# Gate products of an xLSTM step with high and low weights in one stationary array, and the first two query evacuations ahead of the gate rows

## The chip, the core and the metric

The kernel is one program on one core of a Trainium2 chip. The metric is the device time of one execution in microseconds (us). TensorE (PE in the profile, with its weight loads as PEld) multiplies, VectorE (DVE) and ScalarE (ACT) do elementwise work, GpSimd (POOL) does some of it and issues a few transfers, and SyncE (SP) issues most transfers.

## The reference

A decoder step of two layers over 512 prompt tokens and 32 sample tokens (8 sequences of 4), width 1024, all in float32. Layer 0 mixes tokens with an mLSTM (8 heads), layer 1 with a short gated convolution, and each is followed by a squared-ReLU MLP. Every sub-layer has an RMS norm with shift, scale and gate from a conditioning vector (`ada_w`). What the change touches is the gate part of the mLSTM projection: 16 of the columns of `mlstm_w_in`.

```python
def mlstm_mixer(h, C0, n0, m0, w_in, b_gates, g_head, w_out):
    p = (h @ w_in).astype(jnp.float32)
    q = p[..., :hk]
    k = p[..., hk:2 * hk] * (DK_A ** -0.5)
    ...
    gates = p[..., 2 * hk + 2 * D_MODEL:] + b_gates.astype(jnp.float32)
    ig = gates[..., :H_A]
    lf = jax.nn.log_sigmoid(gates[..., H_A:])
    ...
```

The input gates `ig` and the log forget gates `lf` then go through running sums and running maxima over the tokens, which give the decay rows of every head.

## The kernel before

**Tiles.** Activations lie transposed: 8 channel blocks of 128 partitions, each with 544 columns (two halves of 272, which are 256 prompt tokens and 16 sample tokens). A product in full precision is made of three products of rounded parts. The high part of a weight tile is `wh`, the low part `wl = raw - wh`; those of the activations are `Xh` and `Xl`. A weight tile of 128 output channels is 8 channel blocks times (wh·Xh, wh·Xl, wl·Xh) times two halves, which makes 48 matmuls into one of two slots of the accumulator tensor `G`.

**Supply.** SP fetches a raw tile (512 KB) into one of two buffers, ACT rounds it (`hi`, L596) into one of four slots, and POOL subtracts (`lo`, L1102), after which the raw buffer is free for the tile two further on. The tiles of the first stage are the queries and keys, numbers 0 to 7 (T_QK); values (8 to 15), output gates (16 to 23) and so on follow.

**The head of the program.** TensorE turns the input, then makes the first products of `ada_w` (`ada_pair`, 32 small matmuls each, L2153), which give shift and scale of the first norm. DVE and ACT write `Xh` and `Xl` in two groups of four blocks. `gates(k)` (L2240) multiplies block k by the gate weights `gh` (high) and `gl` (low), each 40 columns wide with the input gates at columns 0 to 7 and the forget gates at 32 to 39; three products times two halves, into banks `B5` and `B7`. TensorE does `gates(0)` to `gates(3)`, two ada pairs, and then tiles 0 and 1 together (`head_pair`, matmuls of L1994): blocks 0 to 3 of tile 0, two ada pairs, blocks 0 to 3 of tile 1, and from block 4 on block k of both with `gates(k)` behind it. After that come one ada pair on two tiles of `aring`, tiles 2 and 3 (matmuls of L1968), one ada pair, tiles 4 and 5, and so on. The data of each of these ada pairs are refilled by ACT, which issues the transfers (L471).

**Behind the gates.** DVE adds the bias (L1606, L1607) and makes the absolute value (L1609, semaphore `s_rv`), ACT takes exponential and logarithm (L909, L910), and DVE makes the sums and maxima (L1612 to L1630, second count of `s_rv`).

**What sets the order around the change.** Each engine does its instructions in the order written. In ACT's program, behind the first norm: `hi(2)`, `hi(3)`, then the wait for `s_rv`, L909 and L910, `hi(4)`, the evacuation of tile 0 (`to_qk`, L713 and L714, which empties the slot of `G`), that of tile 1, a refill of two ada tiles, `hi(5)`. Tile 2 uses the slot of tile 0, so TensorE waits for tile 0's evacuation before it. Four tiles later `rows_prompt` waits on ACT for the second count of `s_rv`, behind the evacuation of tile 4.

Of the kernel before, what the change touches and what calls it, by code (L numbers as in the profile page):

```python
# [13 lines left out]
F32 = mybir.dt.float32  # L14
F32R = mybir.dt.float32r
ALU = mybir.AluOpType
ACT = mybir.ActivationFunctionType
AX = mybir.AxisListType

P = 128  # L20
D = 1024
KT = D // P
SEQ, SB, ST = 512, 8, 4
PH, SH = SEQ // 2, SB * ST // 2
HALF = PH + SH
# [3 lines left out]
H, DK, DV = 8, 64, 128  # L29
# [8 lines left out]
SLOTS, RAWS, ADAS, LEAD = 4, 2, 2, 3  # L38
# [12 lines left out]
T_QK, T_V, T_O, T_WOUT, T_MLP0, T_MLP0L, T_MLP0_LAST = 0, 8, 16, 24, 32, 48, 80  # L51
T_CG, T_XT, T_BG, T_COUT, T_MLP1, T_MLP1_LAST, T_END = 96, 104, 112, 120, 128, 176, 192
G_QK, G_V, G_O, G_WOUT, G_MLP0, G_MLP0L, G_MLP0_LAST = 0, 8, 16, 24, 32, 48, 80
# [87 lines left out]
def build_program(nc, ins, outs):  # L141
    ctx = ExitStack()
    with ctx:
# [3 lines left out]
        def sb(name, shape, dt=F32, at=None):  # L147
            n = 4
            for s in shape[1:]:
                n *= s  # L150
            n = (n + 31) // 32 * 32
            if at is None:
                at = mark["at"]
                mark["at"] += n
            return nc.alloc_sbuf_tensor_at(name, shape, dt, offset=at)

        def region(nbytes):
            at = mark["at"]
            mark["at"] += (nbytes + 31) // 32 * 32
            return at  # L160

        def sem(name):
            return ctx.enter_context(nc.semaphore(name))

        ROW = TOK * 4
# [16 lines left out]
        Xh = sb("Xh", [P, KT, TOK], F32R)  # L182
        Xl = sb("Xl", [P, KT, TOK], F32R)
# [38 lines left out]
        at_sq = region(6 * ROW)  # L222
# [13 lines left out]
        bgate = sb("bgate", [P, 1])  # L236
# [4 lines left out]
        xr = sb("xr", [P, TOK], at=at_n + 2 * ROW)  # L241
# [14 lines left out]
        at_f = region(2 * 4 * ROW + KT * ROW + NJ * H * DK * 4)  # L256
# [9 lines left out]
        rows_all = sb("rows_all", [H, 6, TOK], at=at_f + 8 * ROW)  # L266
        rows = [rows_all[:, i, :] for i in range(6)]
        erow = sb("erow", [H, SEQ - P], at=at_f + 14 * ROW)
        gw = 8 * 40 * 4
        graw = sb("graw", [P, KT, 40], at=at_f + 14 * ROW)  # L270
        gh = sb("gh", [P, KT, 40], F32R, at=at_f + 14 * ROW + gw)
        gl = sb("gl", [P, KT, 40], F32R, at=at_f + 14 * ROW + 2 * gw)
        crow = sb("crow", [NSEQ, D], at=at_f)
        parrow0 = sb("parrow0", [P, P], at=at_f + 12288)
        parrow1 = sb("parrow1", [40, P], at=at_f + 12288 + 512)
# [94 lines left out]
        s_gs = sem("gates_split")  # L370
# [207 lines left out]
        def _(act):  # L578
            chain = Count(act, s_a)

            def hi(t, j=None, per=0):

                if t >= T_END:
                    return
                if fast_of(t) is not None:
                    hi_group(fast_of(t)[1], 0, t - fast_of(t)[1])
                    return
                raw_wait(act, t)
                if t >= SLOTS and fast_of(t - SLOTS) is not None:
                    v, u = fast_of(t - SLOTS)  # L590
                    act.wait_ge(s_pu, NP * (PAIRS * v + 3) + min(2 * (t - u - KT) + 2, NP))
                elif t >= SLOTS:
                    act.wait_ge(s_used, at(t - SLOTS + 1, j, per))
                else:
                    act.wait_ge(s_au, 8)
                nc.scalar.activation(wh[:, t % SLOTS], raw_of(t), ACT.Copy).then_inc(s_hi, 1)  # L596
# [129 lines left out]
            def ada_next(k):  # L726

                act.wait_ge(s_au, 2 * (k + 1))
                for a in range(2 * (k + 1), min(2 * (k + 2), BATCH * KT)):
                    ada_fetch(nc.scalar, a)  # L730
# [21 lines left out]
            def raw_hi(n, k):  # L752

                act.wait_ge(s_gn, n)
                act.wait_ge(s_dr, done((0, G_WOUT, G_MLP0_LAST + 8, G_COUT)[n] + k + 1))
                nc.scalar.activation(prompt(XP[n][0][:, k, :]), prompt(xT[:, k, :]), ACT.Identity, scale=gain[:, k, 0:1])\
                    .then_inc(s_xph, 1)
# [67 lines left out]
            def mixed(t0, g0, n, evac, j=None, per_t=0, per_g=0, per_n=0, after={}, ada_after=ADA_AFTER, raws=None):  # L825

                for m in range(KT):
                    t = t0 + m
                    if t != T_QK and m != 1:
                        hi(t + LEAD, j, per_t)  # L830
                    if m == 0:
                        hi(t + 1 + LEAD, j, per_t)
                    if evac is not None:
                        evac(t, g0 + m, j, per_t, per_g)
                    if m in after:
                        after[m]()
                    if raws is not None and m:
                        raw_hi(raws, m - 1)
                    if m in ada_after:
                        ada_next(4 * n + ada_after[m])  # L840
# [47 lines left out]
            for j in range(NJ + 1):  # L888
# [4 lines left out]
                last = nc.scalar.activation(xsq[j % 2][0:n, :], xin[0:n, j, :], ACT.Square, accum_out=rms[0:n, 1, j:j + 1])  # L893
# [3 lines left out]
                nc.scalar.activation(prompt(xT[:, k, :]), G[:, k % 4, :].rearrange("p (h c) -> p h c", h=2),  # L897
                                     ACT.Copy).then_inc(s_xe, 1)
            act.wait_ge(s_gin, 80)
            nc.scalar.activation(gh[:, :, :], graw[:, :, :], ACT.Copy).then_inc(s_gs, 1)  # L900
            first_norm_hi(0)
            first_norm_hi(1)
            hi(2)
# [1 line left out]

            nc.scalar.dma_start(xspill, xT[:, :, :].rearrange("p k c -> p (k c)")).then_inc(s_spill, 16)

            act.wait_ge(s_rv, 1)
            chain.link(nc.scalar.activation(rows[1][:, :], rows[0][:, :], ACT.Exp, scale=-1.0))  # L909
            nc.scalar.activation(rows[2][:, :], rows[1][:, :], ACT.Ln, bias=1.0).then_inc(s_ra, 1)  # L910
# [152 lines left out]
            for i, bank in enumerate((B4, B6)):  # L1063
                last = nc.scalar.activation(urows[:, i * 512:(i + 1) * 512], bank[0:2 * NSEQ, :], ACT.Copy)
# [15 lines left out]
            for j, bank in enumerate((B4, B5, B6, B7)):  # L1080
                last = nc.scalar.activation(yrow[:, j, 0:HALF_D], bank, ACT.Copy)
# [140 lines left out]
        def _(dve):  # L1222
            chain = Count(dve, s_v)
            V = nc.vector
# [365 lines left out]
                                       sample(xr[:, :]).unsqueeze(1).broadcast_to((P, KT, 2, SH)), ALU.mult))  # L1590
            scaled_x(range(4))
            dve.wait_ge(s_gs, 1)
            V.tensor_tensor(gl[:, :, :], graw[:, :, :], gh[:, :, :].bitcast(F32), ALU.subtract).then_inc(s_gs, 1)
            first_norm(0)
            first_norm_low(0)
            scaled_x(range(4, KT))
# [5 lines left out]
            R = [r[:, :] for r in rows]  # L1602
            lf = sqb[0:H, :]
            for hf, bank in enumerate((B5, B7)):
                cols = slice(hf * HALF, (hf + 1) * HALF)
                V.tensor_scalar(R[3][:, cols], bank[0:H, 0:HALF], bgate[0:H, :], None, ALU.add)  # L1606
                V.tensor_scalar(R[4][:, cols], bank[32:32 + H, 0:HALF], bgate[32:32 + H, :], None, ALU.add)  # L1607
            chain.link(V.memset(xr[0:H, :], 1.0))
            V.scalar_tensor_tensor(R[0], R[4], -1.0, R[4], ALU.mult, ALU.max).then_inc(s_rv, 1)  # L1609
            dve.wait_ge(s_ra, 1)  # L1610
# [160 lines left out]
            for h2 in range(2):  # L1771
                pr = slice(DK * h2, DK * (h2 + 1))
                for b in range(SB):
                    last = V.tensor_copy(qbd[pr, :, b, NS * h2 + ST * b:NS * h2 + ST * (b + 1)], qe[pr, :, ST * b:ST * (b + 1)])
# [3 lines left out]
            for h2 in range(2):  # L1778
                pick = lambda ap: ap.rearrange("p (a h) t -> p a h t", h=2)[:, :, h2, :]
                last = V.scalar_tensor_tensor(  # L1780
                    pick(probs_s[:, :, :])[:, :, NS * h2:NS * (h2 + 1)],
                    (B7, B6)[h2][0:NS, 0:H // 2 * NS].rearrange("p (a t) -> p a t", t=NS), KS,
                    pick(dec_s[:, :, :]), ALU.mult, ALU.mult)
# [160 lines left out]
            for half, bank in enumerate((B7, B6)):  # L1944
                last = V.tensor_scalar(yrow_s[:, half * HALF_D:(half + 1) * HALF_D], bank[0:NS, :], rms[0:NS, 1, NJ:NJ + 1], None, ALU.mult)
# [4 lines left out]
        def _(pe):  # L1950
            mm = nc.tensor.matmul

            def turn(out, in_, n):
                return nc.tensor.transpose(out, in_, ident[0:n, 0:n])  # L1954
# [250 lines left out]
            for k in range(KT):  # L2205
                last = turn(B5[:, k * NSEQ:(k + 1) * NSEQ], crow[:, k * P:(k + 1) * P], NSEQ)
# [7 lines left out]
            for k in range(KT):  # L2214
                last = turn(B6[:, k * NS:(k + 1) * NS], xin[0:NS, NJ, k * P:(k + 1) * P], NS)
            last.then_inc(s_xst, 1)
            for k in range(KT):
                if k >= 4:
                    pe.wait_ge(s_xe, k - 3)
                if k == 5:  # L2220
# [4 lines left out]
                    for hf, bank in enumerate((B5, B7)):  # L2225
                        last = mm(bank[:, PH:HALF], ones[:, :], diag[:, NJ, hf * SH:(hf + 1) * SH], start=True, stop=True)
                    last.then_inc(s_root, 1)
                for jt in range(NJ):
                    last = turn(G[:, k % 4, jt * P:(jt + 1) * P], xin[:, jt, k * P:(k + 1) * P], P)
# [9 lines left out]

            def gates(k):  # L2240
                pe.wait_ge(s_kx, X_NORM0 + k + 1)
                for w, x, st, en in ((gh, Xh, k == 0, False), (gh, Xl, False, False), (gl, Xh, False, k == KT - 1)):
                    for hf, bank in enumerate((B5, B7)):
                        last = mm(bank[0:40, 0:HALF], w[:, k, :], x[:, k, hf * HALF:(hf + 1) * HALF], start=st, stop=en)
                if k == KT - 1:
                    last.then_inc(s_gp, 1)

# [219 lines left out]
            for q in range(QUARTERS - 1):  # L2467
                t, g = T_MLP0L + 16 * q, G_MLP0L + 16 * q
# [17 lines left out]
            for k in range(KT):  # L2486
                last = mm((B4, B6)[k // 4][0:2 * NSEQ, (k % 4) * P:(k % 4 + 1) * P], ulast[:, k, :], ident[:, :],
                          start=True, stop=True, is_transpose=True)
# [3 lines left out]
            for q in range(QUARTERS - 1):  # L2492
                t, g = T_MLP1 + 16 * q, G_MLP1 + 16 * q
# [13 lines left out]
            def turn_samples(m):  # L2507
                return turn((B7, B6)[m // 4][0:NS, m % 4 * P:(m % 4 + 1) * P], fin_s[:, m, :], P)

            t, g = T_MLP1_LAST + 8, G_MLP1_LAST + 8  # L2510
            fast_down(T_MLP1_LAST, t, g, Hh, Hl)
            for m in range(2, KT):
                tile(t + m, g + m, Hh, Hl, None, 0, 0)
                if m == 5:
                    pe.wait_ge(s_ulo, 1)
                    pe.wait_ge(s_fy, 4)
                    for n in range(4):
                        last = turn_rows((B4, B5, B6, B7), n)
# [7 lines left out]
            for m in range(KT - 1):  # L2526
                last = turn_samples(m)
# [36 lines left out]
```

## Time and profile before

| | us |
|---|---|
| median of 3 runs | 1311.68 |
| lowest and highest | 1310.95, 1312.01 |
| profiled execution | 1311.63 |
| its span in the trace | 1309.9 |
| TensorE busy in it | 1271.6 |

1.73 us of the profiled execution lie outside the span. The page also gives 11305 matmuls and a mean granted clock of 0.99 of full speed. Times in the trace count from the span's start.

### The profile page before, as it was taken

How to read it: one execution, taken by the hardware profiler on the slowest of the kernel's cores; microseconds unless marked ns; L12 is line 12 of the kernel's file. 1: busy time of each engine (PE TensorE's matmuls, PEld its weight loads, DVE VectorE, ACT ScalarE, POOL GpSimd, SP SyncE). 2: the span in 40 equal slices, each digit the busy share in tenths (PEclk: the TensorE clock that was granted, in tenths of full speed). 3: DMA queues.
4: the chain of work that ended last, by engine and by line, in shares of the span. 5: the costliest groups of instructions: out<-in, count | busy, mean ns of one | idle time of the engine just before them, and what ended most of it. 6: DMA issues, size and time to landing. Idle time of an engine off the chain costs nothing.

```text
span 1309.9 us, 26367 instructions
## 1 busy us (share of the span) xinstructions
PE 1271.6 (97%) x11305; PEld 1246.2 (95%) x11305; DVE 772.5 (59%) x1306; ACT 504.3 (38%) x793; POOL 366.8 (28%) x184
## 2 busy tenths in 40 slices
PE   4799999999999999999999999999999999999996
PEld 4799999999999999999999999999999999999996
DVE  4523445668748643643659809859858743824764
ACT  5332453222542551551462322213362561642721
POOL 2333434342300041042045245435310041050050
PEclk9899999999999999999999999999999999999998
DMA  9748214654366574574553233323132242342321
GB/s 322 236 147 200 80 55 122 223 156 143 114 192 195 158 229 129 155 232 130 151 174 97 66 97 86 93 83 96 51 97 81 66 132 63 97 131 63 97 65 69
DMA packets 242526, 169.34 MB, mean 129 GB/s; under 512 B 5851, under 2 KB 217055, under 8 KB 242282
## 3 DMA queue, kind: packets, MB, share of 16 engines
q1 hardware_dynamic: 215946, 121.33, 32.5%
q10 hardware_dynamic: 26304, 46.27, 10.7%
q8 instruction: 89, 1.46, 0.5%
q14 instruction: 27, 0.22, 0.1%
q0 software_dynamic: 160, 0.07, 0.0%
HBM read 160.70 MB, written 6.94 MB: 128 GB/s over the span
## 4 chain that ended last, share of the span: by engine, by line
PE 82%; DVE 10%; issue 3%; DMA 2%; ACT 2%; POOL 0%; SPq 0%; POOLq 0%; ACTq 0%; DVEq 0%
PE G L1968 38%; PE G L2088 19%; PE G L1994 10%; PE G L2124 6%; PE B L2153 3%; DVE hb L1448 1%; PE B L1954 1%; DVE small_s L1893 1%; DVE acc L1288 1%; DMA raw<-in_mlp_w_down 1%; DVE yc L1892 1%; DVE Xl L1462 1%; DMA xin<-in_x_sample 1%; PE B L2353 1%; PE B L2365 1%
## 5 line engine op out<-in xcount | busy, mean ns | idle before, releaser
L1102 POOL TENSOR_TENSOR wl<-raw,wh 128x1024 fp32r<-128x1024 f32 x128 | 325.6, 2553 | 789.5 <-ACT wh L596 786.6
L596 ACT ACTIVATE wh<-raw 128x1024 fp32r<-128x1024 f32 x144 | 151.9, 1055 | 274.1 <-PE G L1968 147.2
L1968 PE MATMUL G<-Hh,wh 128*128 128x272 f32 x864 | 179.3, 289 | 0.0
L1968 PE MATMUL G<-Hh,wl 128*128 128x272 f32 x864 | 178.3, 288 | 0.0
L1968 PE MATMUL G<-Hl,wh 128*128 128x272 f32 x864 | 178.3, 288 | 0.0
L1968 PE MATMUL G<-Xh,wh 128*128 128x272 f32 x640 | 137.4, 296 | 6.7 <-ACT qT L714 6.7
L1968 PEld LDWEIGHTS G<-Hh,wh 128*128 128x128 f32 x864 | 135.5, 188 | 1.0 <-issue 1.0
L1968 PEld LDWEIGHTS G<-Hl,wh 128*128 128x128 f32 x864 | 135.8, 189 | 0.0
L1968 PEld LDWEIGHTS G<-Hh,wl 128*128 128x128 f32 x864 | 135.0, 189 | 0.0
L1968 PE MATMUL G<-Xl,wh 128*128 128x272 f32 x640 | 133.0, 289 | 0.0
L1968 PE MATMUL G<-Xh,wl 128*128 128x272 f32 x640 | 132.4, 288 | 0.0
L1267 DVE TENSOR_TENSOR small_s<-G,modT 128x32 f32<-128x32 f32 x80 | 15.2, 189 | 178.1 <-PE G L1968 121.4
L1968 PEld LDWEIGHTS G<-Xh,wh 128*128 128x128 f32 x640 | 100.5, 190 | 10.9 <-ACT wh L596 6.9
L2088 PE MATMUL G<-Th,wl 128*128 128x272 f32 x384 | 110.8, 288 | 0.0
L2088 PE MATMUL G<-Tl,wh 128*128 128x272 f32 x384 | 110.6, 288 | 0.0
L2088 PE MATMUL G<-Th,wh 128*128 128x272 f32 x384 | 110.3, 287 | 0.0
L1968 PEld LDWEIGHTS G<-Xl,wh 128*128 128x128 f32 x640 | 101.5, 190 | 0.0
L1968 PEld LDWEIGHTS G<-Xh,wl 128*128 128x128 f32 x640 | 100.9, 190 | 0.0
L612 ACT ACTIVATE wh<-raw 128x512 fp32r<-128x512 f32 (+1 forms) x48 | 40.5, 843 | 98.1 <-PE G L1968 57.7
L612 ACT ACTIVATE wh<-wsum 128x1024 fp32r<-128x1024 f32 x48 | 50.7, 1056 | 68.4 <-PE G L1968 48.8
L2088 PEld LDWEIGHTS G<-Th,wh 128*128 128x128 f32 x384 | 72.5, 189 | 0.0
L2088 PEld LDWEIGHTS G<-Tl,wh 128*128 128x128 f32 x384 | 72.3, 188 | 0.0
(397 smaller groups left out, 2768.9 us busy)
## 6 DMA issues: line engine op xcount, KB each, us to landing
raw<-in_mlp_w_up SPq DMA_DIRECT2D x64, 512.0 KB, 4.2
raw<-in_mlp_w_down SPq DMA_DIRECT2D x64, 512.0 KB, 4.3
aring<-in_ada_w ACTq DMA_DIRECT2D x60, 512.0 KB, 5.1
raw<-in_mlstm_w_in SPq DMA_DIRECT2D x24, 512.0 KB, 4.3
raw<-in_conv_w_in SPq DMA_DIRECT2D x24, 512.0 KB, 3.7
free_l<-in_ada_w ACTq DMA_DIRECT2D x20, 256.0 KB, 6.9
early<-in_ada_w SPq DMA_DIRECT2D x8, 512.0 KB, 11.9
raw<-in_mlstm_w_out SPq DMA_DIRECT2D x8, 512.0 KB, 4.7
```

The source lines that it names most:

```text
L596: nc.scalar.activation(wh[:, t % SLOTS], raw_of(t), ACT.Copy).then_inc(s_hi, 1)
L612: nc.scalar.activation(wh8[:, b0:b1, :], src, ACT.Copy).then_inc(s_whi, 1)
L1102: nc.gpsimd.tensor_tensor(wl[:, t % SLOTS], raw_of(t), wh[:, t % SLOTS].bitcast(F32), ALU.subtract).then_inc(s_lo, 1)
L1267: mid(V.tensor_tensor(small_s[:, :].rearrange("p (h b t) -> p h b t", h=2, t=ST), ps[:, :, PH:HALF].rearrange("p h (b t) -> p h b t", t=ST ...
L1288: ins_ = V.tensor_tensor(acc[:, :], acc[:, :], sqb[:, :], ALU.add)
L1448: V.scalar_tensor_tensor(prompt(hb[k % 2][:, :]), prompt(xT[:, k, :]), gain[:, k, 0:1], prompt(xr[:, :]), ALU.mult, ALU.mult).then_inc(s_h ...
L1462: V.scalar_tensor_tensor(prompt(xl[:, k, :]), prompt(hb[k % 2][:, :]), modT[:, sh, k, 0:1], prompt(xh[:, k, :].bitcast(F32)), ALU.add, ALU ...
L1968: last = mm(G[:, 2 * (g % 2) + hf, 0:HALF], w[:, s, k, :], x[:, k, hf * HALF:(hf + 1) * HALF], start=st, stop=en)
L1994: last = mm(G[:, q + hf, 0:width], w[:, s, k, :], x[:, k, hf * width:(hf + 1) * width], start=st, stop=en)
L2088: last = mm(G[:, bank, 0:HALF], w[:, s, r, :], y, start=st, stop=en, skip_group_check=True)
L2124: last = mm(G[:, q + hf, 0:HALF], w[:, s, k, :], x[:, k, hf * HALF:(hf + 1) * HALF], start=st, stop=en)
L2153: last = mm(out[GW * g:GW * (g + 1), P * quad:P * (quad + 1)], cpad[:, kk, :], columns, start=(kk == 0), stop=(kk == KT - 1), tile_positio ...
```

## The change

The high and the low gate weights lie side by side in one array `gboth` of 104 columns: high at 0 to 39, low at 64 to 103, zeros between (ACT writes columns 40 to 63 from the zero columns of `graw`). One product with `Xh` gives both high·Xh (rows 0 to 39 of the bank) and low·Xh (rows 64 to 103); the second, with `Xl`, gives high·Xl and, in addition, low·Xl. DVE copies rows 64 to 71 and 96 to 103 of each half to `xr` and adds them with the bias. `graw` lies in another place. And ACT evacuates tiles 0 and 1 and rounds tile 4 ahead of the wait for the gate rows, not behind it.

```diff
-        graw = sb("graw", [P, KT, 40], at=at_f + 14 * ROW)
-        gh = sb("gh", [P, KT, 40], F32R, at=at_f + 14 * ROW + gw)
-        gl = sb("gl", [P, KT, 40], F32R, at=at_f + 14 * ROW + 2 * gw)
+        graw = sb("graw", [P, KT, 40], at=at_sq)
+        gboth = sb("gboth", [P, KT, 104], F32R, at=at_f + 14 * ROW)
+        gh, gl = gboth[:, :, 0:40], gboth[:, :, 64:104]
...
-                    if m == 0:
+                    if m == 0 and t != T_QK:
                         hi(t + 1 + LEAD, j, per_t)
-                    if evac is not None:
+                    if evac is not None and t >= T_QK + 2:
                         evac(t, g0 + m, j, per_t, per_g)
...
+            nc.scalar.activation(gboth[:, :, 40:64], graw[:, :, H:32], ACT.Copy)
+            nc.scalar.activation(gh, graw[:, :, :], ACT.Copy).then_inc(s_gs, 1)
...
+            for m in range(2):
+                to_qk(T_QK + m, G_QK + m, None, 0, 0)
+            hi(T_QK + SLOTS)
             act.wait_ge(s_rv, 1)
...
-                V.tensor_scalar(R[3][:, cols], bank[0:H, 0:HALF], bgate[0:H, :], None, ALU.add)
-                V.tensor_scalar(R[4][:, cols], bank[32:32 + H, 0:HALF], bgate[32:32 + H, :], None, ALU.add)
+                V.tensor_copy(xr[0:H, cols], bank[64:64 + H, 0:HALF])
+                chain.link(V.tensor_copy(xr[32:32 + H, cols], bank[96:96 + H, 0:HALF]))
+                V.scalar_tensor_tensor(R[3][:, cols], bank[0:H, 0:HALF], bgate[0:H, :], xr[0:H, cols], ALU.add, ALU.add)
+                chain.link(V.scalar_tensor_tensor(R[4][:, cols], bank[32:32 + H, 0:HALF], bgate[32:32 + H, :], xr[32:32 + H, cols],
+                                                  ALU.add, ALU.add))
...
-                for w, x, st, en in ((gh, Xh, k == 0, False), (gh, Xl, False, False), (gl, Xh, False, k == KT - 1)):
+                for x, st, en in ((Xh, k == 0, False), (Xl, False, k == KT - 1)):
                     for hf, bank in enumerate((B5, B7)):
-                        last = mm(bank[0:40, 0:HALF], w[:, k, :], x[:, k, hf * HALF:(hf + 1) * HALF], start=st, stop=en)
+                        last = mm(bank[0:104, 0:HALF], gboth[:, k, :], x[:, k, hf * HALF:(hf + 1) * HALF], start=st, stop=en)
```

ACT behind the first norm, before. `wh<-raw` is the rounding of a weight tile (here tiles 2 and 3 together, then 4, then 5), L713 and L714 are an evacuation, and the semaphore `rows_vector` is `s_rv`:

```order
29 L596 ACTIVATE wh<-raw 128x1024 [waits ada_tile_used,raw_in0]
30 L596 ACTIVATE wh<-raw 128x1024 [waits ada_tile_used,raw_in1]
31 L906 DMA xspill<-xT 128x4352
32 L909 ACTIVATE rows_all<-rows_all 8x544 [waits rows_vector]
33 L910 ACT_TABLE_LOAD
34 L910 ACTIVATE rows_all<-rows_all 8x544 [waits scalar_chain]
35 L596 ACTIVATE wh<-raw 128x1024 [waits tile_used,raw_in0]
36 L713 ACTIVATE qs<-G 128x32 [waits tile_used]
37 L714 ACTIVATE qT<-G 128x512
38 L713 ACTIVATE qs<-G 128x32 [waits tile_used]
39 L714 ACTIVATE qT<-G 128x512
40 L471 DMA aring<-in_ada_w 128x2x512 [waits ada_tile_used]
```

The same stretch of ACT now:

```order
30 L595 ACTIVATE wh<-raw 128x1024 [waits ada_tile_used,raw_in0]
31 L595 ACTIVATE wh<-raw 128x1024 [waits ada_tile_used,raw_in1]
32 L906 DMA xspill<-xT 128x4352
33 L712 ACTIVATE qs<-G 128x32 [waits tile_used]
34 L713 ACTIVATE qT<-G 128x512
35 L712 ACTIVATE qs<-G 128x32 [waits tile_used]
36 L713 ACTIVATE qT<-G 128x512
37 L595 ACTIVATE wh<-raw 128x1024 [waits tile_used,raw_in0]
38 L912 ACTIVATE rows_all<-rows_all 8x544 [waits rows_vector]
39 L913 ACT_TABLE_LOAD
40 L913 ACTIVATE rows_all<-rows_all 8x544 [waits scalar_chain]
41 L470 DMA aring<-in_ada_w 128x2x512 [waits ada_tile_used]
```

Both evacuations and the rounding of tile 4 moved ahead of the wait for `rows_vector`; the refill of `aring` stays behind it.

DVE between the last block of `Xl` and the absolute value, before:

```order
43 L1384 TENSOR_TENSOR Xl<-hb_114,Xh 128x2x256
44 L1606 TENSOR_SCALAR rows_all<-B,bgate 8x272
45 L1607 TENSOR_SCALAR rows_all<-B,bgate 8x272
46 L1606 TENSOR_SCALAR rows_all<-B,bgate 8x272
47 L1607 TENSOR_SCALAR rows_all<-B,bgate 8x272
48 L1608 MEMSET xr 8x544
49 L1609 SCALAR_TENSOR_TENSOR rows_all<-rows_all 8x544
```

And now:

```order
43 L1387 TENSOR_TENSOR Xl<-hb_114,Xh 128x2x256
44 L1609 COPY xr<-B 8x272
45 L1610 COPY xr<-B 8x272
46 L1611 SCALAR_TENSOR_TENSOR rows_all<-B,bgate,xr 8x272
47 L1612 SCALAR_TENSOR_TENSOR rows_all<-B,bgate,xr 8x272
48 L1609 COPY xr<-B 8x272
49 L1610 COPY xr<-B 8x272
50 L1611 SCALAR_TENSOR_TENSOR rows_all<-B,bgate,xr 8x272
51 L1612 SCALAR_TENSOR_TENSOR rows_all<-B,bgate,xr 8x272
52 L1614 MEMSET xr 8x544
53 L1615 SCALAR_TENSOR_TENSOR rows_all<-rows_all 8x544
```

Four instructions became eight ahead of the absolute value.

## Rows read from the trace of the kernel before

**Rows 1.** The page's head, and TensorE's line: busy us, share, instructions.

```profile
span 1309.9 us, 26367 instructions
PE 1271.6 (97%) x11305; PEld 1246.2 (95%) x11305; DVE 772.5 (59%) x1306; ACT 504.3 (38%) x793; POOL 366.8 (28%) x184
```

**Rows 2.** Waits of TensorE over the span: us in total, times, longest.

```profile
PE G L1968 <- ACT qT L714: 6.7, 1, 6.7
PE B L2244 <- DVE Xl L1384: 5.7, 2, 4.3
```

**Rows 3.** Timeline, TensorE, tiles 1 to 5: start, duration, line, operands, [idle before].

```profile
55.49 0.41 PE L2244 MATMUL B<-Xh,gl 128*40 128x272 f32 x2
55.83 1.08 PE L2153 MATMUL B<-aring,cpad 128*32 128x128 f32 x32
63.56 0.79 PE L1968 MATMUL G<-Xh,wh 128*128 128x272 f32 x2 [6.65 <-ACT qT L714]
...
77.92 1.08 PE L2153 MATMUL B<-aring,cpad 128*32 128x128 f32 x32
78.93 0.52 PE L1968 MATMUL G<-Xh,wh 128*128 128x272 f32 x2
...
91.15 1.08 PE L2153 MATMUL B<-aring,cpad 128*32 128x128 f32 x32
```

**Rows 4.** Timeline, ACT and its transfer queue (ACTq), behind the gates.

```profile
59.29 0.66 ACT L909 ACTIVATE rows_all<-rows_all 8x544 f32<-8x544 f32 x1 [8.28 <-DVE rows_all L1609]
...
61.28 0.92 ACTq L471 DMA_DIRECT2D aring<-in_ada_w  x2
61.82 1.04 ACT L596 ACTIVATE wh<-raw 128x1024 fp32r<-128x1024 f32 x1
...
62.85 0.57 ACT L714 ACTIVATE qT<-G 128x512 f32<-128x512 f32 x1
```

**Rows 5.** Timeline, DVE, from the gates' product to the second count of `s_rv`.

```profile
55.94 0.49 DVE L1606 TENSOR_SCALAR rows_all<-B,bgate 8x272 f32<-8x272 f32 x1 [6.09 <-PE B L2244]
...
58.55 0.71 DVE L1609 SCALAR_TENSOR_TENSOR rows_all<-rows_all 8x544 f32<-8x544 f32 x1
...
72.58 0.42 DVE L1630 TENSOR_SCALAR rows_all<-rows_all 8x544 f32<-8x544 f32 x1
```

**Rows 6.** Stretches: us, busy (x) per engine, granted clock, DMA share, GB/s.

```profile
37.00:38.00 1.00, 1.00 (x32) 0.94 (x28) 0.66 (x2) 0.00 (x0) 0.00 (x0) 0.65 0.99 371
...
61.00:63.00 2.00, 0.00 (x0) 0.00 (x0) 1.02 (x2) 1.99 (x5) 0.06 (x1) 0.65 0.28 40
...
68.00:69.00 1.00, 1.00 (x8) 1.00 (x8) 0.86 (x5) 0.00 (x0) 0.26 (x1) 0.79 0.75 226
```

**Rows 7.** Timeline, TensorE, from `gates(2)` to the ada pairs behind `gates(3)`.

```profile
32.53 0.68 PE L2244 MATMUL B<-Xh,gh 128*40 128x272 f32 x2 [1.38 <-DVE Xl L1384]
...
34.81 0.66 PE L2244 MATMUL B<-Xh,gl 128*40 128x272 f32 x2
35.40 3.05 PE L2153 MATMUL B<-early_x,cpad 128*32 128x128 f32 x64
```

**Rows 8.** Timeline, TensorE, `gates(4)` and the tile products behind it.

```profile
48.24 0.41 PE L2244 MATMUL B<-Xh,gh 128*40 128x272 f32 x2
...
49.00 0.41 PE L1994 MATMUL G<-Xh,wh 128*128 128x272 f32 x2
...
49.75 0.42 PE L1994 MATMUL G<-Xh,wh 128*128 128x272 f32 x2
```

**Rows 9.** Timeline, the splitting of the gate weights on ACT, then on DVE.

```profile
20.93 0.48 ACT L900 ACTIVATE gh<-graw 128x320 fp32r<-128x320 f32 x1
```

```profile
23.42 0.49 DVE L1593 TENSOR_TENSOR gl<-graw,gh 128x320 fp32r<-128x320 f32 x1
```

**Rows 10.** Timeline, POOL: low parts of tiles 2 and 3; landings of `raw`, of `aring`.

```profile
50.15 4.76 POOL L1102 TENSOR_TENSOR wl<-raw,wh 128x1024 fp32r<-128x1024 f32 x2 [14.85 <-ACT wh L596]
```

```profile
DMA to landing us min/median/max: 3.8/4.8/12.9
```

```profile
DMA to landing us min/median/max: 4.0/4.9/12.1
```

More of the change, by code:

```diff
@@ L268, in build_program @@
         erow = sb("erow", [H, SEQ - P], at=at_f + 14 * ROW)
-        gw = 8 * 40 * 4
-        graw = sb("graw", [P, KT, 40], at=at_f + 14 * ROW)
-        gh = sb("gh", [P, KT, 40], F32R, at=at_f + 14 * ROW + gw)
-        gl = sb("gl", [P, KT, 40], F32R, at=at_f + 14 * ROW + 2 * gw)
+        graw = sb("graw", [P, KT, 40], at=at_sq)
+        gboth = sb("gboth", [P, KT, 104], F32R, at=at_f + 14 * ROW)
+        gh, gl = gboth[:, :, 0:40], gboth[:, :, 64:104]
         crow = sb("crow", [NSEQ, D], at=at_f)
@@ L899, in _ @@
             act.wait_ge(s_gin, 80)
-            nc.scalar.activation(gh[:, :, :], graw[:, :, :], ACT.Copy).then_inc(s_gs, 1)
+            nc.scalar.activation(gboth[:, :, 40:64], graw[:, :, H:32], ACT.Copy)
+            nc.scalar.activation(gh, graw[:, :, :], ACT.Copy).then_inc(s_gs, 1)
             first_norm_hi(0)
@@ L1592, in _ @@
             dve.wait_ge(s_gs, 1)
-            V.tensor_tensor(gl[:, :, :], graw[:, :, :], gh[:, :, :].bitcast(F32), ALU.subtract).then_inc(s_gs, 1)
+            V.tensor_tensor(gl, graw[:, :, :], gh.bitcast(F32), ALU.subtract).then_inc(s_gs, 1)
             first_norm(0)
```

## The prediction, made before the changed kernel ran

> **What bounds the kernel now.** I read the head of the page first: TensorE is busy in 1271.6 of 1309.9 us [rows 1], so only what shortens TensorE's own work or its waits can count. The list of TensorE's waits comes next. Its longest entry is one wait of 6.7 us for an evacuation by ACT [rows 2]; the 5.7 us for `Xl` are two waits, 4.3 us before `gates(0)` and 1.38 us before `gates(2)` [rows 2, 7]. Third, the timeline of TensorE shows where the long one lies: the ada pair behind tiles 0 and 1 ends at 55.83 + 1.08 = 56.91, and tile 2 starts at 63.56 [rows 3]. Fourth, ACT's timeline shows why. ACT was idle for 8.28 us until DVE's L1609, did the gate rows from 59.29 to about 61.9, then rounded tile 4, and only then emptied tile 0's slot at 62.85 + 0.57 = 63.42 [rows 4]. The evacuation had nothing to wait for but its place in the queue. Fifth, the granted clock: 0.65 as the mean of 61 to 63 and 0.79 of 68 to 69 [rows 6], so the clock fell from 2.4 to 1.2 GHz at about 61.6, after some 5 us without a matmul, and came back at about 68.4, 4.9 us after TensorE had resumed. All later work is paced by TensorE, so what is won here moves the end.
>
> **The wait before tile 2.** Removed: tile 0 ends half a block pair before tile 1, ACT evacuates it at once (0.57 us for the prompt columns [rows 4] and less for the few sample columns), while TensorE still has tile 1's last block (0.75), the gates and the ada pair (1.08) to do, over 2 us in all. Gain 6.65 us. What could be late next? The low part of tile 2 needs POOL until about 52.5 and that of tile 3 until 54.91 [rows 10], tile 2 would start near 55.2. Neither waits.
>
> **The clock behind it.** Tiles 2 and 3 took 77.92 - 63.56 = 14.36 us, tiles 4 and 5 with the same 96 matmuls 91.15 - 78.93 = 12.22 [rows 3]. The difference, 2.14 us, is work at 1.2 GHz, and it goes with the wait, since TensorE then works without a gap from 32.53 on. First the row, then the rule: the fall came in a gap of 6.65 us, and the gap of 1.38 us at 31 us fell into a stretch that was at 1.2 GHz anyway [rows 3, 6, 7]. The Trainium skill (TensorE: Matmul & The Clock Gate, the section on HAM oscillation) warns that idle gaps between bursts put the array back to half clock; the trace agrees, and by the rule as by the row the 2.14 us are won.
>
> **The gates at full clock.** `gates(4)` to `gates(7)` lose two of six matmuls each. Three pairs took 49.00 - 48.24 = 0.76 us with 40 weight columns, and three pairs with 128 columns took 49.75 - 49.00 = 0.75 [rows 8]. So a pair costs 0.25 us whichever width, 104 lies between, and 4 pairs less are 1.00 us. By the Trainium skill (TensorE: Matmul & The Clock Gate, LDWEIGHTS) a weight load grows with its columns, about columns / 1.2 ns, an estimate of 54 ns more for 104 than for 40 columns. Were that in the open for 32 loads, 1.7 us of the gain would be lost; the equal pairs of [rows 8] say that it is covered, and I take nothing for it.
>
> **The gates at low clock.** `gates(0)` and `gates(1)` get shorter but `gates(2)` still starts at 32.53, when its `Xl` is there: nothing won. `gates(2)` and `gates(3)` lose 2 pairs at (34.81 - 32.53) / 5 = 0.456, that is 0.91 us [rows 7]. The clock rose at about 37.65 [rows 6], while the ada pairs of 35.40 to 38.45 ran [rows 7]. If it rises at the same moment, work at low clock is replaced by work at high clock, and 0.91 us at the low are worth 0.46 at the high; if it rises with the work done, all 0.91 count. I take 0.68, the middle. Everything downstream (ada products, shift, `Xh`, `Xl` of blocks 4 to 7) follows TensorE's ada pairs and moves along.
>
> **What is added.** ACT copies 24 zero columns per block before `gh`: no more than the 0.48 us of the larger copy at 20.93, which ended 2 us before DVE used it at 23.42 [rows 9]: 0. DVE does eight instructions instead of four. L1606 took 0.49 and started 0.50 apart (the four ended at 57.94, the absolute value at 59.26) [rows 5]. Bounds for one of the four new ones: 0.3, since fewer columns than the 0.71 of 544 [rows 5] hardly go lower, and 0.71 itself. I take 0.50, the nearest in shape, and 0.1 for the links: 2.1 us more. The gates' product ends 1.68 us earlier (1.00 + 0.68), so the first count of `s_rv` comes at 59.26 - 1.68 + 2.1 = 59.7, practically where it was. Nobody on TensorE's path waits for it now. Queued behind that wait on ACT are L909 and L910, the refill of `aring`, `hi(5)` and tile 2's evacuation. `hi(5)` ends near 63.4, tile 5 is due at about 74.5. Tile 2 is finished at about 61.2 and its evacuation ends at about 64.1, tile 4 wants the slot at 68.4. Rounding tile 4 must wait for its raw tile, fetched when POOL is done with tile 2 (52.5) and landing 4.8 us later [rows 10], about 57.3; it ends by 58.4, before `s_rv`. The sums and maxima ended at 73.00, 13.7 us after the first count [rows 5]; now at about 73.4, and ACT asks for them behind tile 4's evacuation, near 75.3. Slack 2 us, cost 0.
>
> **The sum.** 6.65 + 2.14 + 1.00 + 0.68 = 10.47 us of 1311.63, which is 1301.2. The profiled execution lies 0.05 us from the median of the three, so I leave it at that. One unknown of execution to execution is the moment at which the clock rises in the head; the spread of the runs, 1.06 us from lowest to highest, holds it, and I use it as 0.7 to either side.
>
> **Rival 1, the ada refill becomes the wait.** Its place is the ada pair behind tile 3. That pair is now due at 55.2 + 12.2 = 67.4, where it stood at 77.92. Its two tiles are fetched behind L910, at 59.7 + 2.0 = 61.7 (61.28 before [rows 4]), issued over 0.92 us, with 4.9 us to landing [rows 10]: 66.6 to 67.5. Slack was 10 us and is now about none. Against a large cost: the transfer engines are otherwise almost idle then (40 GB/s in 61 to 63 [rows 6]). For one: the raw tile 6 is now fetched at about 61 too, since POOL is done with tile 4 earlier, and three 512 KB tiles at the 371 GB/s of [rows 6] need 4.2 us. With each new DVE instruction at 0.71 the refill is another 0.9 us later. Price 0.4 to 2.5 us, time 1301.6 to 1303.7; a typical value 1302.6.
>
> **Rival 2, the gate rows become the wait.** If the sums and maxima end after 75.3, ACT stands before `rows_prompt`, with the rounding of tile 8 and tile 5's evacuation behind it. Tile 7 wants that slot near 87.7, so even 5 us late would cost nothing. It decides only from more than 8 us late. Price up to 3 us: 1304. Little speaks for it.
>
> **Rival 3, slower than before: the raw supply becomes the bound.** Two raw buffers serve all tiles up to the MLP. One buffer's cycle is landing 4.8 + rounding 1.04 [rows 4] + low part 4.76 / 2 = 2.4 [rows 10], together 8.2 us, for which TensorE gives two tiles, 12.05. It decides from a landing of 8.6 us. With TensorE 10.5 us ahead, the state loads and refills meet the same raw tiles. The highest landing in the trace is 12.9 us [rows 10]; at that value each two tiles take 16.3 us and 6 tiles lose 13 us, which gives 1301.2 + 13 = 1314. Against it: the 12.9 is of the crowded first 30 us, the median is 4.8, and after tile 2 TensorE never waited for weights.
>
> **Rival 4, the change doesn't do what it says.** The order on ACT shows the evacuations ahead of the wait, so this is only about the gap: if tile 2 waited for something that the trace names wrongly (its weights also came into question, and they were there at 54.91), all but 1.7 us would be lost, 1309.9.
>
> **Chances.** Forecast 0.73, rival 1 0.18, rival 2 0.02, rival 3 0.03, rival 4 0.02; the last 0.02 for the clock rising later in the head by more than the spread. The forecast reaches from 1301.2 - 0.7 - 0.23 - 0.7 (the last for DVE's and the ada stage's own surprises in my favour) = 1299.6 to 1302.0; rival 1 takes the upper end to 1303.7. The range 1299.6 to 1303.7 holds about 9 in 10 of the cases, and cutting it further would cut into rival 1. 0.2% is 2.6 us, about what a measurement of this kernel can tell from no change: faster 0.95, same 0.02 (rival 4, 0.14% faster), slower 0.03 (rival 3).
>
> **What would show it.** In the profile of after: no entry of the evacuation in TensorE's waits; granted clock 1.00 from about 38 us on; tile 2 at 55.2 and the ada pair behind tile 3 at 67.4, with a gap before it if rival 1 holds; 32 gate matmuls, pairs at 0.25 us once the clock is up; L1615 on DVE ending at about 59.7; ACT not idle before `rows_prompt` beyond its evacuation (rival 2). From tile 4 on every stage should start 10.5 us earlier. The prediction is wrong if a gap returns further on, or if the 104 columns stretch the pairs.

## The result, and the profile after

The changed kernel took 1304.0 us, the median of 4 executions from 1301.8 to 1305.57; the kernel before beside it took 1311.79. The ratio is 0.9941 with a 95% interval of 0.9924 to 0.9957, so it is faster by 0.4 to 0.8%. Forecast were 1301.2 us and 1299.6 to 1303.7: the sign was right, and the median lies 2.8 us above the forecast and 0.3 above the range. The profiled execution of after took 1301.80, 0.6 from the forecast, and was the fastest of the four. So one execution went as predicted, and the median didn't.

The head of after's page, to be held beside [rows 1]:

```profile
span 1300.0 us, 26340 instructions
PE 1267.4 (97%) x11289; PEld 1242.6 (96%) x11289; DVE 778.9 (60%) x1310; ACT 504.5 (39%) x794; POOL 366.9 (28%) x184
```

TensorE has 16 matmuls less. Of its waits (total us, times, longest), where [rows 2] had 6.7 us for the evacuation, these are what the argument needs:

```profile
PE B L2250 <- DVE Xl L1387: 6.2, 2, 4.3
...
PE B L2159 <- DMA aring<-in_ada_w: 0.3, 1, 0.3
```

The wait for ACT is gone. The wait before `gates(2)` is 1.99 instead of 1.38, as the shorter `gates(0)` and `gates(1)` end earlier. The timeline of TensorE, where [rows 3] stood, and the granted clock of the head (third number from the right end; us, busy per engine, clock, DMA share, GB/s), as in [rows 6]:

```profile
32.33 0.78 PE L2250 MATMUL B<-Xh,gboth 128*104 128x272 f32 x2 [1.99 <-DVE Xl L1387]
...
54.07 1.08 PE L2159 MATMUL B<-aring,cpad 128*32 128x128 f32 x32
55.09 0.52 PE L1974 MATMUL G<-Xh,wh 128*128 128x272 f32 x2
...
67.30 1.08 PE L2159 MATMUL B<-aring,cpad 128*32 128x128 f32 x32
```

```profile
34.00:36.00 2.00, 2.00 (x35) 1.60 (x37) 2.00 (x2) 0.00 (x0) 1.10 (x1) 0.50 1.05 385
36.00:38.00 2.00, 2.00 (x43) 1.71 (x36) 1.60 (x4) 0.00 (x0) 0.00 (x0) 0.70 1.05 385
```

Tile 2 starts at 55.09 (forecast 55.2), the ada pair behind tile 3 at 67.30 (67.4), with no gap before either. The clock rises in the head near 37.2 and falls again only at 1293.3, behind TensorE's last matmul. On DVE, ACT and POOL the gate rows did take longer than forecast:

```profile
57.23 2.40 POOL L1105 TENSOR_TENSOR wl<-raw,wh 128x1024 fp32r<-128x1024 f32 x1 [3.08 <-ACT wh L595]
```

```profile
57.56 0.49 DVE L1612 SCALAR_TENSOR_TENSOR rows_all<-B,bgate,xr 8x272 f32<-8x272 f32 x1
...
58.77 1.44 DVE L1615 SCALAR_TENSOR_TENSOR rows_all<-rows_all 8x544 f32<-8x544 f32 x1
...
72.14 2.18 DVE L1634 TENSOR_TENSOR rows_all<-m0row,rows_all 8x8 f32<-8x8 f32 x1
```

```profile
76.88 1.28 ACT L918 ACT_TABLE_LOAD   x1 [1.56 <-DVE rows_all L1636]
```

L1615 is the absolute value that took 0.71 in [rows 5]. It now runs while POOL makes the low part of tile 4, which starts earlier, and takes 1.44. Further on, L1634, a step on 8x8 elements, takes 2.18 beside POOL's next subtraction (71.57 to 74.29), where the same instruction took 0.16 before. The sums and maxima end at 76.0, not 73.4, and ACT waits 1.56 us for them before `rows_prompt`. In this execution TensorE doesn't notice.

### The profile page after: what moved, and what is told of

The parts are those of the page before. It is cut to its first block, busy times and chain, and to the rows that moved or that the text cites. A ratio compares the mean times of both kernels' runs of the same rounds, so it can differ in the third digit from the quotient of the medians.

```text
span 1300.0 us, 26340 instructions
## 1 busy us (share of the span) xinstructions
PE 1267.4 (97%) x11289; PEld 1242.6 (96%) x11289; DVE 778.9 (60%) x1310; ACT 504.5 (39%) x794; POOL 366.9 (28%) x184
## 4 chain that ended last, share of the span: by engine, by line
PE 82%; DVE 10%; issue 3%; DMA 2%; ACT 2%; POOL 0%; SPq 0%; POOLq 0%; DVEq 0%; ACTq 0%
PE G L1974 39%; PE G L2094 20%; PE G L2000 10%; PE G L2130 6%; PE B L2159 3%; PE B L1960 1%; DVE small_s L1899 1%; DVE acc L1291 1%; DVE hb L1451 1%; DMA raw<-in_mlp_w_down 1%; DVE yc L1898 1%; DMA xin<-in_x_sample 1%; DVE Xl L1465 1%; PE B L2359 1%; ACT wh L595 1%
```

## The experiments

Times of executions are the device times; medians, unless said otherwise. All runs of one heading shared a chip and the runs of the kernel before beside them.

### What the parts do

**e1** is the changed kernel again. **e2** has only ACT's new order:

```diff
-                    if m == 0:
+                    if m == 0 and t != T_QK:
                         hi(t + 1 + LEAD, j, per_t)
-                    if evac is not None:
+                    if evac is not None and t >= T_QK + 2:
...
+            for m in range(2):
+                to_qk(T_QK + m, G_QK + m, None, 0, 0)
+            hi(T_QK + SLOTS)
             act.wait_ge(s_rv, 1)
```

**e3** has only the gates (`gboth`, two products, DVE's eight instructions). **e4** is the changed kernel with

```diff
             hi(T_QK + SLOTS)
+            ada_next(8)
             act.wait_ge(s_rv, 1)
```

and without the same refill further back.

> The changed kernel once more, as it is, to see how its executions are spread: 1301.8, 1302.5, 1305.5 and 1305.6 us so far. Theory H (the clock in the head): TensorE's first rise to full clock comes later in some executions; the two groups stay, about 1302 and 1305.6, and the mean granted clock is lower in the slow one by 0.002 or more. Theory D (the refill of the ada tiles lands late): two groups too, but at the same mean clock. Theory N (no groups, a broad spread): values in between.

> The kernel before with ACT's new order alone; the gates keep three products a block and the four additions on DVE. By the terms of my sum the wait and the slow clock behind it go (6.65 + 2.14 us) and the gates stay: 1311.7 - 8.8 = 1302.9 in an undisturbed execution. Theory D: the refill is due 1.7 us later here and issued 0.8 earlier than in the changed kernel, so nearly all executions are undisturbed and the median lies near 1303, below the changed kernel's 1304. Theory H: the same two groups as in the changed kernel, 1303 and 1306.5.

> The kernel before with the two gate products alone; ACT keeps its old order, so TensorE waits for the gate rows as before. TensorE's work is 1.68 us shorter, but tile 2 now waits for a DVE chain that is 2.1 us longer. My reading: tile 2 starts at 63.56 - 1.68 + 2.2 = 64.1, so 0.4 to 0.6 us slower than before, 1312.2. A rival, that the gates' products pay even so: 1310.0. Theory H and D both expect a spread as narrow as before's.

> The changed kernel, with the refill of the two ada tiles behind tiles 0 and 1 issued ahead of ACT's wait for the gate rows, some 4 us earlier. Theory D: the group at 1305.6 goes, all executions 1301.2 to 1302.5. Theory H: nothing changes, two groups at 1302 and 1305.6.

| | median | lowest, highest | executions | ratio to before, 95% |
|---|---|---|---|---|
| before | 1310.27 | 1308.22, 1312.24 | 11 | |
| e1 after | 1303.84 | 1301.23, 1306.23 | 6 | 0.9951 (0.9937, 0.9964) |
| e2 order only | 1302.0 | 1300.61, 1303.46 | 5 | 0.9939 (0.9927, 0.9951) |
| e3 gates only | 1314.21 | 1312.25, 1315.82 | 5 | 1.0033 (1.0021, 1.0044) |
| e4 early refill | 1302.35 | 1301.16, 1302.51 | 5 | 0.9938 (0.9926, 0.995) |

Three things follow. The order alone gives the whole gain, and no less than both together. The gates alone cost 3.9 us, where I had expected 0.5. And one execution is not like another: the kernel before, which showed 1310.95 to 1312.01 in the runs that I started from, ranges over 4 us, and its executions with a mean clock of 0.993 or more lie below 1310.3. The "groups" that I saw in after were not groups; values lie in between (theory N, a spread that the kernel before has as well). In e3's profile, an execution of 1312.25 us, the wait before tile 2 had grown from 6.7 to

```profile
PE G L1971 <- ACT qT L713: 8.6, 1, 8.6
```

since tile 2 there waits for a longer DVE chain behind shorter gates. That is not a loss by itself: from `gates(0)` to the ada pair behind tile 3 e3 takes 49.67 us and my first profile of before 49.68, so the shorter gates and the longer wait cancel. Another 1.8 us are lost behind that, 0.8 of them in a wait for ada data at 98.7. The profile was the fastest of e3's five executions, so what makes up the rest of the 3.9 us is not shown. That e4 had no execution above 1302.51 looked like theory D, by which the late refill of the ada ring makes the slower executions; but it had five of them.

### The clock in the head

Two runs keep TensorE at work in the two gaps, on top of the early refill, once with two gate products (**e5**) and once with three (**e6**, 5 matmuls in the second gap):

```diff
+            def keep_busy(n):
+                for _ in range(n):
+                    mm(G[:, 3, 0:HALF], ident[:, :], xT[:, 0, 0:HALF], start=True, stop=True)
+
+            keep_busy(8)
             for k in range(4):
                 gates(k)
+                if k == 1:
+                    keep_busy(6)
```

**e7** and **e8** are the changed kernel again, each for a profile.

> The kernel with the early refill (two gate products a block), with TensorE kept at work in the two gaps of the head: 8 matmuls of 272 float32 columns into a free bank ahead of gates(0), 6 more between gates(1) and gates(2); their results are overwritten and nobody reads them. Theory H (the loss and the spread are the clock's, which stays at 1.2 GHz from about 28 to 37 or 39 us): the granted clock stays at 1.00 through the head, gates(3), two ada pairs and the first tile products run at full speed, 1.5 to 2.5 us faster than the early refill (1302.35), 1300.2, and the spread shrinks to under 1 us. Rival: the gaps hold TensorE for other reasons and the work between them is paced by Xl: no gain, 1302.3.

> The same (early refill, TensorE kept at work, 5 matmuls in the second gap) with the old three gate products a block and four additions. With the clock out of play the gates' own price shows: by my sum, six blocks times one pair of 0.25 us more for three products, so 1.0 to 1.5 us slower than the run with two products. Rival (two products cost something besides the clock, by DVE's longer chain): as fast or faster than with two.

> The changed kernel, one look, to find an execution of the slow group (1305 to 1306 us) in a profile. Theory D: in such an execution TensorE waits 3 us or more for the aring data before the ada pair behind tile 3. Theory H: the clock rises at 40 us or later, and no wait is new.

> The same, a second look; as in the first, theory D expects a wait for aring in an execution above 1305 us, theory H a later rise of the clock.

e5 took 1300.55 (1299.90 to 1301.68, 4 executions, ratio 0.9922, 0.9908 to 0.9936), e6 1300.99 (1300.83 to 1302.41, 5 executions), before beside them 1311.39. The clock stayed at full speed through the head in both; e6:

```profile
30.00:32.00 2.00, 2.00 (x13) 1.72 (x12) 1.43 (x2) 2.00 (x4) 1.92 (x1) 1.00 1.05 386
```

From the start of `gates(0)` to the first product on `aring` e5 takes 23.98 us and e6 25.35: with the clock up, two products save 1.4 us there, close to the 1.5 that 0.25 us per pair gives for six blocks. The medians differ by 0.4, and I can't tell that from nothing with four and five executions. e7 and e8 took 1302.84 and 1301.30; neither lies in the tail, so they say nothing on D.

### The refill, and the tail

**e9** puts the refill further back (behind `hi(5)` and tile 2's evacuation), **e10** is the changed kernel a third time, **e11** the early refill again, **e12** the early refill with three gate products and no added matmuls.

> The changed kernel with the refill of the two ada tiles moved further back, behind the rounding of tile 5 and the evacuation of tile 2, so issued near 63.5 us, not at 60.9. Theory D (the refill has no slack left in the changed kernel): 63.5 + 0.9 + 4.9 = 69.3 against 67.3, TensorE waits 2 us or more before the ada pair behind tile 3, and the median rises by as much or more, 1305.5 to 1307. Theory H (only the clock in the head): 2 us are within what the pair can stand, 1303.8 as the changed kernel.

> The changed kernel once more beside the next two, on the same chip. Theory D: some executions above 1304.5 again, as 5 of 12 so far, median near 1303.5. Theory H: a spread like that of the run with the early refill.

> The early refill once more (two gate products). Theory D: none above 1303, median 1302.3, as in its first run. Theory H: as spread as the changed kernel beside it.

> The early refill with the three gate products and four additions of before, no added matmuls. If two products are worth their 1.5 us with the clock as it comes: 1303.8. If the three products hold the clock's rise earlier in some executions (in the order-only run it was at full speed from 32 us), the gain is given back: 1302.0 to 1302.5, no difference.

| | median | lowest, highest | executions |
|---|---|---|---|
| before | 1310.73 | 1308.26, 1312.58 | 12 |
| e9 refill late | 1304.67 | 1303.05, 1305.59 | 4 |
| e10 after | 1303.53 | 1301.15, 1308.43 | 6 |
| e11 early refill | 1303.88 | 1301.22, 1309.6 | 7 |
| e12 early refill, three products | 1302.26 | 1301.59, 1304.24 | 5 |

Theory D falls twice. e11 has a tail as long as the changed kernel's, although the refill is early. And e9's profile, an execution of 1305.59 us, shows the ada pair behind tile 3 at 68.67, 13.22 us behind the pair before it, as in all other profiles of the new order: the refill is in time. It was a weaker test than meant, though: the refill was issued at 63.66, 8.2 us behind the pair before, where it is 6.9 in after (60.94 against 54.07), so 1.3 us later and not 3. e9's median of 1304.67 lies between the two expectations; with four executions it decides nothing. Where did e9's profiled execution lose its 3.8 us against after's, then? 1.4 in the head (`gates(0)` starts 1.0 us later, and the stretch to the aring product is 26.44 against 26.02), and 2.5 far behind the change, nearly all of it beside this wait:

```profile
PE B L2161 <- DMA batch<-in_ada_w: 2.1, 1, 2.1
```

The wait for the batch data is at 364 us, and behind it the clock is at half from 366.7 to 370.1. e11's profile, 1303.88 us, shows the same on a smaller wait: an ada pair whose second half waits 0.62 us for its data (first row), then stretches of 1 to 3 us, with the clock falling near 273.3 and back near 276.7:

```profile
270.87 0.65 PE L2160 MATMUL B<-aring,cpad 128*32 128x128 f32 x16 [0.62 <-DMA aring<-in_ada_w]
```

```profile
270.00:271.00 1.00, 0.38 (x17) 0.14 (x8) 0.78 (x2) 0.12 (x1) 0.00 (x0) 1.00 0.02 8
...
273.00:276.00 3.00, 3.00 (x15) 3.00 (x16) 1.65 (x6) 0.00 (x0) 2.93 (x2) 0.55 0.83 269
276.00:278.00 2.00, 2.00 (x15) 2.00 (x15) 0.00 (x0) 0.00 (x0) 1.29 (x1) 0.83 0.25 92
```

### The kernel before, and the order with TensorE at work

**e13** and **e14** are the kernel before again, each for a profile. **e15** is the kernel before with the added matmuls (8 and 5), **e16** the order alone with them.

> The kernel before, as it is, one look. From its ada pair at 91.15 to its first product on batch data at 372.62 the profile that I had took 281.5 us; variants took 281.7 to 284.2. Theory S (the later waits are in both kernels): some look at before takes 282 us or more, with a wait for aring or batch data or a dip of the granted clock between 250 and 390 us. Theory M (they come with the change): 281.5 again, no such wait.

> The kernel before, a second look, with the same expectations: theory S a stretch of 282 us or more in at least one of the two, theory M 281.5 in both.

> The kernel before with the added matmuls in the two gaps of the head (8 and 5 of 272 float32 columns, results overwritten), nothing else. Theory H for the head: the clock stays up, 2 us faster than before's median beside it, the wait of 6.7 us before tile 2 stays and the clock falls in it as before. If the head's clock were hidden by what comes after: no change.

> The new order alone (three gate products, the refill behind the gate rows) with the added matmuls in the head. If neither the second gate product nor the early refill matters: 1301.0 as the run with three products and the early refill (1300.99). If the refill matters: 1302 or more, with executions above 1303.5.

e13 took 1311.74 and e14 1310.48, and the stretch of 281.5 us was 281.7 and 282.1 in them, with a wait for batch data of 0.4 in e14 and for aring of 0.3 in e13. So such waits are in the kernel before too (theory S), of the size that after's profile has; no dip of the clock there fell into these two profiles. e14's head is the find. Its granted clock was already full at 32 us, where mine was at half until 37.7:

```profile
30.00:32.00 2.00, 1.68 (x8) 1.00 (x6) 1.43 (x2) 2.00 (x3) 1.94 (x1) 0.51 1.06 390
32.00:34.00 2.00, 0.94 (x8) 0.87 (x9) 2.00 (x3) 1.04 (x2) 1.34 (x2) 1.00 1.05 385
```

```profile
28.77 0.65 PE L2244 MATMUL B<-Xh,gh 128*40 128x272 f32 x2 [4.28 <-DVE Xl L1384]
...
33.06 0.45 PE L2244 MATMUL B<-Xh,gh 128*40 128x272 f32 x2 [1.38 <-DVE Xl L1384]
33.34 0.41 PE L2244 MATMUL B<-Xl,gh 128*40 128x272 f32 x2
```

The same program, the same work ahead of the rise (`gates(0)` and `gates(1)` with three products), and `gates(2)` at 0.25 to 0.28 us a pair, not 0.456 as in [rows 7]. From `gates(0)` to the first aring product e14 needs 25.27 us, the profile that I started from 27.59, e13 27.53.

e15: 1309.6 (1308.30 to 1312.64, 11 executions), ratio 0.9994 (0.9985 to 1.0003) to before's 1310.25; the 2 us that I expected did not come. Its stretch is 25.34 us, that of e14: for executions that rise early anyway there is nothing to win. The mean clock of the executions bears this out. In the profiles of before it is 0.990 and 0.991 where the clock rose late, and 0.993 in e14. Of the 49 executions of before with a clock on record beside the experiments and in e13 and e14, 27 have 0.993 or more, with a median of 1309.7, and 22 less, with a median of 1311.7; e15's median is that of the first sort. e16: 1300.86 (1299.48 to 1301.22, 5 executions), ratio 0.9923 (0.991 to 0.9937). It needs neither the second gate product nor the early refill, and with e5 and e6 it has the lowest medians that I found; the three spread over 1.6 to 1.8 us. Which of them is best I can't tell. Taken together, the ten executions of e6 and e16 have a median of 1300.9, the ten of e2 and e12, which lack only the added matmuls, 1302.2, though on other chips.

## Why the prediction was right or wrong, point by point

**The wait before tile 2 (6.65 us): right.** Gone, in every profile with the new order; nothing took its place. e2 alone beats before by 8.3 us.

**The clock behind it (2.14 us): right in size.** Tiles 2 and 3 take 67.30 - 55.09 = 12.21 us in after, forecast 12.22, and 13.22 us with the ada pair before them in all profiles of the new order. Both terms together were forecast at 8.79 us; the order without the gates (e2 and e12, 10 executions) has a median of 1302.2, 8.5 below before's 1310.6.

**The gates (1.00 + 0.68 us): the step that failed.** I had priced them from one profile, with the moment of the clock's rise as noise. In the profiled execution it came true: 26.02 us from `gates(0)` to the aring product against 27.59, 1.57 less. Over executions it did not: the order with three products has the median of 1302.2, the changed kernel (18 executions: the first four, e1, e7, e8, e10) 1303.3. The ranges overlap (1300.6 to 1304.2, and 1301.2 to 1308.4), so that two products are slower isn't shown; but 1.7 us faster, as forecast, they are not. Two things stand in the way.

First, the row that I priced against was of one sort of execution. Of five profiles with three products and without added matmuls (before, e13, e14, e2, e12) three took 27.3 to 27.6 us for the stretch and two, e2 and e14, 25.2 to 25.3. Of the nine with two products (after, e1, e3, e4, e7 to e11) none had the clock back before 36 us, and the stretch was 25.9 to 26.7: 0.7 to 1.4 us more than in the early sort. In twelve of these fourteen profiles the clock stays at half for 10.2 us in the head, in e2 and e14 for 3.4. The mean clock tells the same of executions without a profile. With the new order it is 0.996 in e2's profile (early) and 0.993 in e12's (late); 5 of the 10 executions of e2 and e12 have 0.995 or more, and none of the 34 with the new order and two products (after, e1, e4, e7 to e11). So the early rise is what two products lose. In the prediction's terms, I took the moment of the rise as an unknown that the spread of 1.06 us holds and took the middle of two values; it moved the stretch by 2.3 us, and the change itself moved it. Why the early rise doesn't come is inferred: two products leave the gap before `gates(2)` longer, 1.99 us against 1.38. The closest pair is e2 and e9, where the clock fell at 28.8 in both and rose at 32.1 and 39.0. e5 and e6, where the clock is held up and two products are no slower, fit this too. No run changed the gap alone.

Second, DVE's longer chain seems to reach TensorE, by a way that I hadn't looked at. ACT's `rows_prompt` starts 3.65 us ahead of the ada pair behind tile 5 in after and 4.63 ahead in e2, and the refill behind it ends 2.84 us behind that pair's start, against 2.04 in e2. In three of the five profiles of the changed kernel (e1, e8, e10) it ends 2.99 to 3.06 behind, and the ada pair behind tile 6 waits for it; e1's:

```profile
90.57 0.65 PE L2159 MATMUL B<-aring,cpad 128*32 128x128 f32 x16 [0.64 <-DMA aring<-in_ada_w]
```

That costs these executions 0.4 to 0.9 us. No profile with three products has this wait. That the later chain makes the refill late is read from the order of ACT's program; no run changed it alone.

At half clock 104 columns weren't free either: the first pair behind a wait took 0.58 us, against 0.47 with 40 columns. At full clock the pairs are equal, as forecast.

**The base: mis-sized, and it hid a part of the miss.** I took 1311.63 as typical because three runs lay within 1.06 us, and gave 0.7 us to either side for execution to execution. 53 executions of before range from 1308.2 to 1313.2, with a median of 1310.6, and the changed kernel's 18 range over 7.3 us. The same terms from 1310.6 would have given 1300.2, further from what came. The gain is 1310.6 - 1303.3 = 7.3 us and not 10.5; of the 3.1 us that are missing, by the medians, 0.3 belong to the order and 2.8 to the gates. That the median of 18, 1303.3, lies in the range of 1299.6 to 1303.7 is luck: the range went up to there for rival 1, which didn't happen.

**What after loses on top.** The profile of after is 0.6 above the forecast: 80.53 at the ada pair behind tile 5 against 80.68 forecast, so all is there until then (0.2 of it because `gates(0)` started earlier), and 0.67 too late at the first product on the MLP's sums (422.07 against 431.87 - 10.47 = 421.40), by small waits for ada data and weights. From that product to TensorE's last one all 18 profiles, of before and of every variant, take 868.05 to 868.23 us. So what differs between profiled executions lies ahead of it: the start of `gates(0)`, 27.1 to 29.3 us, the clock in the head, and waits for ada and batch data at a few fixed places.

The other executions of the changed kernel lie up to 6.6 us above the profiled one. Six of the 18 have a mean clock of 0.992 or less and all six are above 1304; twelve have 0.993 or more, median 1302.2. e9 and e11 show one way to get there, a wait for data behind 260 us and a stretch of 3.4 us at half clock behind it. Whether such dips are more frequent with the change, as the tail suggests (1308.4 and, with the early refill, 1309.6, against at most 1.5 us above the median of 1311.7 of the slower executions of before), or whether that is chance, stays open: none of the slowest executions was profiled.

**Rival 1 (the refill) was right on the slack and cost nothing.** The pair behind tile 3 never waited. But in after the two landings took 5.4 and 6.2 us, not 4.9, and the second tile landed at 67.6, some 0.2 us before the second half of the pair wanted it. **Rival 2** came by half: DVE's chain was 2.6 us later than forecast at its end and ACT waited 1.56 us. That it would cost TensorE nothing holds for after's profile, and seems wrong for the three above. **Rivals 3 and 4** didn't happen (that TensorE never waits for weights behind tile 2 was not quite so: both kernels have one wait for `wl`, of 0.8 and 0.9 us). **DVE's additions** were priced well one by one (0.43 to 0.49 against 0.50); what I missed were L1615 and L1634 beside POOL, 0.7 and 2.0 us. They come with ACT's new order and not with the gates: in e2, which has the old additions, the absolute value takes 2.37 us.

## What to carry to other kernels

A wait that ends with an evacuation stuck in a queue behind something it doesn't need is won by reordering alone; do that first, and measure each part of a bundled change by itself, since a part that looks like less work can cost. Before pricing by a profiled execution, look at two or three more of the same program: where TensorE works at half clock in a stretch, its rise can come 5 us earlier or later, and a row from one of them is half of the truth. Where the clock starts low behind a gap, useless matmuls in the gap can win time (e6 and e16 against e12 and e2, 1.2 us between the medians); in the kernel before, where by the mean clock about half of the executions rose early anyway and a later gap remained, they won nothing that can be told from noise, and the spread stayed (e15).

## What the hardware showed that I had not expected

The clock's rise in one and the same program: near 32 us in e14, 37.7 in the first profile, with `gates(0)` at 28.77 and 28.24. The Trainium skill (TensorE: Matmul & The Clock Gate, Part 1) says that the moment of the rise differs from execution to execution, and counts the cost as small for a typical kernel; these profiles agree, with 2.3 us for the stretch between them, under 0.2% of the kernel. Here that was larger than the 1.7 us forecast for the gates.

An elementwise instruction on 8 partitions took 1.44 us instead of 0.71 because it ran beside POOL's 128x1024 subtraction: it ended at 60.21, 0.58 us after POOL's 59.63. In e2 the same instruction took 2.37 us beside the same subtraction and ended 0.58 us after it as well, and the 8x8 step of L1634 took 2.18 us instead of 0.16 beside another one. The Trainium skill (SBUF — State Buffer, Who interferes with whom) says that DVE and GpSimd share a pair of ports that only one of them holds at a time; these rows agree.

Matmuls with 104, 128 and 40 weight columns in float32r follow each other at 0.25 us a pair alike at full clock, and at 0.45 at half when they come without a pause. The first pair behind a wait at half clock takes longer with more columns: 0.47 us with 40 and 0.58 with 104 (`gates(2)` of before and of after), 0.59 with 128 (tile 2 of before, 63.56 to 64.15).
